# Opening of a two-layer fp32 decoder trunk: five modulation tiles on TensorE, x second in the load queue, conv rows as 128 rows, small loads from ScalarE

## The reference

```
cond = silu(c)
shift, scale, gate = split(cond @ ada_w[layer] + ada_b[layer], 3)
h = rms_norm(x, norm_w[layer]) * (1 + scale) + shift
x = x + gate * branch(h)
```

## Time and profile before

| | us |
|---|---|
| median of 3 runs | 1510.14 (1509.96 to 1510.31) |
| profiled execution | 1509.85, its span 1508.1 |
| TensorE busy | 1446.5 (96%) |
| VectorE busy | 1105.2 (73%) |
| ScalarE busy | 744.5 (49%) |
| take of a modulation tile (L853) | 188.9 for 148, 1.276 each |
| low part of a granule (L834) | 585.5 for 480, 1.222 each |
| DMA | 361.47 MB, mean 240 GB/s |

### The profile page before, as it was taken

The page is one execution under the profiler, slowest core; times in us unless marked ns, Lnnn a source line. Parts: engine busy times, 40 slices in busy tenths (PEclk is TensorE's granted clock), DMA queues, the critical chain, the costliest instruction groups (busy, mean ns, idle before and its releaser), DMA issues.

```text
span 1508.1 us, 19057 instructions
## 1 busy us (share of the span) xinstructions
PE 1446.5 (96%) x6679; PEld 1198.7 (79%) x6679; DVE 1105.2 (73%) x1234; ACT 744.5 (49%) x1002; POOL 41.7 (3%) x78
## 2 busy tenths in 40 slices
PE   2889999999999989899999999999999999999998
PEld 2767888888888867688888888888888888888886
DVE  5999899989898875878766566566566666656657
ACT  3544646454446455544544544544554454554452
POOL 1000110101000000000000000000000000000000
PEclk9999999999999999999999999999999999999999
DMA  9999889998989735798766566556566566566553
GB/s 338 386 393 391 269 282 339 324 327 287 336 294 353 263 114 183 254 310 300 251 184 187 174 191 185 173 189 188 174 194 181 173 191 193 167 189 190 178 182 112
DMA packets 199230, 361.47 MB, mean 240 GB/s; under 512 B 14224, under 2 KB 48360, under 8 KB 199164
## 3 DMA queue, kind: packets, MB, share of 16 engines
q1 hardware_dynamic: 198112, 359.60, 72.3%
q10 hardware_dynamic: 1056, 1.06, 0.2%
HBM read 358.51 MB, written 2.11 MB: 239 GB/s over the span
## 4 chain that ended last, share of the span: by engine, by line
PE 76%; issue 10%; DVE 7%; ACT 3%; DMA 2%; SPq 1%; POOL 0%; ACTq 0%; DVEq 0%; POOLq 0%
PE proj L1336 23%; PE proj L1338 22%; PE proj L1337 22%; DVE ada_acc L853 4%; PE mix L1336 1%; PE mix L1338 1%; PE mix L1337 1%; DVE w_lo L834 1%; DMA raw<-in_att_w_in 1%; DMA ada_more<-in_ada_w 1%; ACT w_hi L563 1%; PE mix L1455 1%; PE mix L1522 1%; PE mix L1570 1%; ACT work L646 1%
## 5 line engine op out<-in xcount | busy, mean ns | idle before, releaser
L834 DVE TENSOR_TENSOR w_lo<-raw,w_hi 128x1024 fp32r<-128x1024 f32 x480 | 585.5, 1222 | 355.5 <-ACT w_hi L563 354.8
L563 ACT ACTIVATE w_hi<-raw 128x1024 fp32r<-128x1024 f32 x480 | 507.4, 1061 | 682.5 <-PE proj L1338 570.5
L1336 PE MATMUL proj<-w_hi,h_hi 128*128 128x512 f32 x1472 | 583.7, 397 | 7.1 <-DVE h_lo L906 3.9
L1338 PE MATMUL proj<-w_hi,h_lo 128*128 128x512 f32 x1472 | 575.2, 391 | 0.0
L1337 PE MATMUL proj<-w_lo,h_hi 128*128 128x512 f32 x1472 | 574.6, 390 | 0.0
L1336 PEld LDWEIGHTS proj<-w_hi,h_hi 128*128 128x128 f32 x1472 | 277.7, 189 | 66.9 <-issue 9.1
L1338 PEld LDWEIGHTS proj<-w_hi,h_lo 128*128 128x128 f32 x1472 | 277.1, 188 | 58.6
L1337 PEld LDWEIGHTS proj<-w_lo,h_hi 128*128 128x128 f32 x1472 | 277.7, 189 | 57.6 <-issue 1.4
L853 DVE SCALAR_TENSOR_TENSOR ada_acc<-ada_raw,cond,ada_acc 128x1024 f32<-128x1024 f32 x148 | 188.9, 1276 | 2.8 <-DMA ada_raw<-in_ada_w 1.8
L1336 PE MATMUL proj<-w_hi,y_hi 128*128 128x512 f32 x320 | 126.0, 394 | 1.3 <-DVE stream L1004 1.3
L1338 PE MATMUL proj<-w_hi,y_lo 128*128 128x512 f32 x320 | 124.6, 389 | 0.0
(11 more groups left out here) (202 smaller groups left out, 936.5 us busy)
## 6 DMA issues: line engine op xcount, KB each, us to landing
raw<-in_mlstm_w_in SPq DMA_DIRECT2D x192, 512.0 KB, 3.7
ada_raw<-in_ada_w SPq DMA_DIRECT2D x160, 512.0 KB, 6.0
raw<-in_att_w_in SPq DMA_DIRECT2D x128, 512.0 KB, 7.1
raw<-in_mlstm_w_in SPq DMA_DIRECT2D x128, 256.0 KB, 3.0
raw<-in_mlstm_w_out SPq DMA_DIRECT2D x64, 512.0 KB, 4.3
raw<-in_att_w_out SPq DMA_DIRECT2D x32, 512.0 KB, 6.1
ada_more<-in_ada_w SPq DMA_DIRECT2D x16, 512.0 KB, 10.9
work<-in_ada_w SPq DMA_DIRECT2D x16, 512.0 KB, 10.6
```

The lines of the kernel that those rows point to most:

```text
L563: act.activation(w_hi[:, c % LEAD, :], raw[:, c % LEAD, :], ACT.Copy).then_inc(hi_ready, 1)
L834: dve.tensor_tensor(w_lo[:, c % LEAD, :], raw[:, c % LEAD, :], w_hi[:, c % LEAD, :].bitcast(F32), ALU.subtract).then_inc(lo_ready, 1)
L1336: pe.matmul(out_, a_hi, b_hi, start=start, stop=False, **kw)
L1338: return pe.matmul(out_, a_lo, b_hi, start=False, stop=stop, **kw)
```

## The change

Four things, all in the first 45 us:

1. Tiles 3, 5, 8, 14 and 15 of block 0 are not taken by VectorE. TensorE multiplies each with its condition column: the tile is the stationary operand, eight pieces of 128x128, and `cond[:, t]` the one moving column (`mod_part`). Each of these groups of eight matmuls has eight columns of its own in `mix[3]`, and VectorE adds the six sets of columns with two reduces in `mod_evac`. SyncE waits for TensorE before it fills such a tile's slot again (`slot_free`).
2. x is loaded second, behind tile 0, and ScalarE squares a chunk as soon as it has landed (a semaphore for each chunk). The normalization stands earlier on VectorE, behind the takes of tiles 2 and 4.
3. The conv weights are loaded as 128 rows of 512 B into 128 partitions, turned with one transpose, and no longer lie in `raw`, so SyncE's wait for `conv_turned` is gone.
4. The five small loads (c, constants, `norm_w`, `mlstm_norm_w`, conv weights) are issued by ScalarE.

The core of the diff:

```diff
-        conv_rows = raw[:].rearrange("p l n -> p (l n)")[0:TAPS, 0:2 * QK1]
+        conv_rows = work[:, 9344:9472]
+        BY_PE = {0: (3, 5, 8, 14, 15)}
+        def slot_free(sp, n):
+            if by_pe(n) and n % KT == KT - 1:
+                sp.wait_ge(ada_summed, n // KT + 1)
+            elif by_pe(n):
+                sp.wait_ge(ada_pe, turned(n + 1))
+            else:
+                sp.wait_ge(ada_tile, taken(n + 1))
         def load_ada(sp, n):
...
-            wait(sp, ada_tile, n + 1 - (ADA_START if n < ADA_LATE + ADA_SLOTS else ADA_SLOTS))
+            before = n - (ADA_START if n < ADA_LATE + ADA_SLOTS else ADA_SLOTS)
+            if before >= 0:
+                slot_free(sp, before)
         def sp_program(sp):
-            sp.dma_start(rows_c, c[0].rearrange("(t p) -> t p", p=P)).then_inc(c_in, 16)
-            sp.dma_start(const[:], consts[:, 0:C_COS]).then_inc(consts_in, 16)
-            sp.dma_start(rows_n, norm_w.rearrange("l (t p) -> (l t) p", p=P)).then_inc(c_in, 16)
+            load_ada(sp, 0)
             sp.wait_ge(bias_zeroed, 1)
-            for n in range(KT):
+            sp.dma_start(ada_bias[0:1], ada_rows[0:1, 0:2, 0:NC]).then_inc(ada_bias_in, 16)
+            for q in range(CHUNKS):
+                sp.dma_start(stream[:, :, q * NC:(q + 1) * NC], x_v[:, :, q * NC:(q + 1) * NC]).then_inc(x_in[q], 16)
+            for n in range(1, KT):
                 load_ada(sp, n)
-                if n == 3:
-                    sp.dma_start(rows_v, mlstm_norm_w[0].rearrange("(t p) -> t p", p=P)).then_inc(rows_in, 16)
-                    sp.dma_start(conv_rows, mlstm_conv_w[0]).then_inc(rows_in, 16)
-                for q in X_AFTER.get(n, []):
-                    sp.dma_start(stream[:, :, q * NC:(q + 1) * NC], x_v[:, :, q * NC:(q + 1) * NC]).then_inc(x_in, 16)
-            sp.wait_ge(conv_turned, 1)
         def act_program(act):
+            act.dma_start(rows_c, c[0].rearrange("(t p) -> t p", p=P)).then_inc(c_in, 16)
+            act.dma_start(const[:], consts[:, 0:C_COS]).then_inc(consts_in, 16)
+            act.dma_start(rows_n, norm_w.rearrange("l (t p) -> (l t) p", p=P)).then_inc(c_in, 16)
+            act.dma_start(rows_v, mlstm_norm_w[0].rearrange("(t p) -> t p", p=P)).then_inc(rows_in, 16)
+            act.dma_start(conv_rows, mlstm_conv_w[0].rearrange("k (j p) -> (k j) p", p=P)).then_inc(rows_in, 16)
         def mod_evac(dve, bank, k, layer, b):
-            dve.tensor_copy(shift_flat[:, at], mix[bank][:, 0:4])
+            scale = mix[bank][:, 4:8]
+            if k in BY_PE:
+                sums = mix[bank][:, 0:8 * (1 + len(BY_PE[k]))].rearrange("p (i j) -> p j i", j=8)
+                scale = scale_sum[:]
+                dve.tensor_reduce(scale, sums[:, 4:8], AX.X, ALU.add).then_inc(scale_added, 1)
+                dve.tensor_reduce(shift_flat[:, at], sums[:, 0:4], AX.X, ALU.add)
+                dve.wait_ge(scale_added, list(BY_PE).index(k) + 1)
         def dve_program(dve):
             for n in range(KT):
-                take_ada(dve, n)
-                if n == 8:
+                if not by_pe(n):
+                    take_ada(dve, n)
+                if n == 0:
                     dve.wait_ge(conv_turned, 1)
...
-                if n == 9:
+                if n == 2:
                     norm_sum(dve, 0)
-                if n == 11:
+                if n == 4:
                     norm_scale(dve, 0)
+        def mod_part(pe, k, t):
+            n = k * KT + t
+            at = 8 * (1 + BY_PE[k].index(t))
+            pe.wait_ge(ada_in[slot_of(n)], slot_fills(n) * 16)
+            for j in range(8):
+                op = pe.matmul(mix[3][:, at + j:at + j + 1],
+                               ada_slot[slot_of(n)][:, j // 4, j % 4 * P:(j % 4 + 1) * P],
+                               cond[:, t:t + 1], start=True, stop=True)
         def pe_program(pe):
             pe.wait_ge(cond_ready, 1)
+            mod_part(pe, 0, 3)
+            mod_part(pe, 0, 5)
             pe.wait_ge(xn_act, CHUNKS)
             pe.wait_ge(xn_dve, CHUNKS)
-            for q in range(UNIT):
+            for q in range(4):
                 turn_x(pe, 0, q)
-            pe.wait_ge(xnT_act, 4)
-            mod_sum(pe, 3, 0, 0)
+            mod_part(pe, 0, 8)
+            for q in range(4, UNIT):
+                turn_x(pe, 0, q)
+            mod_taken(pe, 0)
+            mod_part(pe, 0, 14)
+            mod_part(pe, 0, 15)
```

More of the change, by code:

```diff
@@ L289, in build @@
             "consts_in", "rows_in", "norms_in", "gates_in"))
-        x_in, x_again, ones_set, rows_turned = (sem(n) for n in (
-            "x_in", "x_again", "ones_set", "rows_turned"))
+        x_again, ones_set, rows_turned = (sem(n) for n in ("x_again", "ones_set", "rows_turned"))
+        x_in = [ctx.enter_context(nc.semaphore(f"x_in{q}")) for q in range(CHUNKS)]
         cond_ready, rows_out, masks_ready, rope_table = (sem(n) for n in (
@@ L358, in fills, with by_pe, taken, turned @@
             return it * (BODY // LEAD + sum(n % LEAD == c % LEAD for n in body)) + sum(1 + two_loads(n) for n in same)
+        BY_PE = {0: (3, 5, 8, 14, 15)}
+        def by_pe(n):
+            return n % KT in BY_PE.get(n // KT, ())
+        def taken(n):
+            return sum(not by_pe(i) for i in range(n))
+        def turned(n):
+            return sum(by_pe(i) and i % KT < KT - 1 for i in range(n))
         MOD, GATE = 0, 1
@@ L586, in turn_bank @@
         def turn_bank(layer, q):
-            return mix[q % 4] if layer or q < 4 else proj[q // 2 % 2][q % 2]
+            if layer:
+                return mix[q % 4]
+            return [mix[0], mix[1], mix[2], proj[1][1], proj[0][0], proj[0][1], proj[1][0], mix[0]][q]
         def xnT_evac(act, q):
@@ L842, in take_ada @@
             if t:
-                dve.wait_ge(ada_tile, n)
+                dve.wait_ge(ada_tile, taken(n))
                 other = sum_
@@ L1231, in dve_program @@
                 {i + 1: [lambda k=k: mod_evac(dve, 3, k, 1, k - 4)] for i, k in SUM_MOD1.items()},
[L1232 removed]
+                {i: [lambda n=n: take_ada(dve, n) for n in ns if not by_pe(n)] for i, ns in TAKES0.items()},
                 {-4: [lambda: h_rest(dve, 0, 1)]},
@@ L1430, in turn_rows @@
             pe.transpose(proj[0][1][:, 128:160], rows_v, ident[0:32, 0:32])
-            for j in range(2 * QK1 // P):
-                op = pe.transpose(proj[0][1][:, j * TAPS:(j + 1) * TAPS], conv_rows[:, j * P:(j + 1) * P],
-                                  ident[0:TAPS, 0:TAPS])
-            op.then_inc(conv_turned, 1)
+            pe.transpose(proj[0][1][:, 0:P], conv_rows, ident).then_inc(conv_turned, 1)
         def turn_x(pe, layer, q):
@@ L1439, in turn_x @@
             pe.wait_ge(xn_dve, CHUNKS * layer + q // 2 + 1)
+            if layer == 0 and q == 7:
+                pe.wait_ge(xnT_act, 1)
             if layer and q >= 4:
```

42 lines of the change are left out of this document (27 added, 15 removed).

## The result

| | before | after |
|---|---|---|
| median of 20 executions each | 1510.35 us | 1513.20 us |
| ratio | | 1.0017 [1.0009, 1.0025] |
| profiled execution, its span | 1509.85, 1508.1 | 1509.55, 1507.7 |

Forecast were 1506.2 us and a gain of 3.9. One execution of each set (1648.8 and 2987.0 us) lies far off the others, and the ratio leaves it out. The changed kernel's other executions stand in two clusters: nine at 1509.0 to 1511.9, ten at 1513.0 to 1516.9 us. Of those of before, 18 of 19 stand at 1509.3 to 1511.8, one at 1513.8. The profiled execution of the changed kernel is of the lower cluster.

What follows compares the result with a forecast made beforehand. The weight stream was taken as the limit, with VectorE barely keeping up. Stream gain 3.5 plus 0.4 slack gave 3.9 us off 1509.85, 1505.95; with the median 0.29 higher, 1506.2 us, 8-in-10 range 1504.6 to 1508.4.

Steps and rivals of the forecast that it cites:

- A weight stream at its ceiling: Stages from 58 to 120 us: the DMA engines are busy without a pause at 394 GB/s, taken as the most possible.
- forecast A: Main forecast: the weight stream limits how much of the opening's lead reaches the end; -3.9 us, 1506.2, chance 0.54.
- the 0.47 us between raw 15's two parts: Near 83 us: time from the high part's end to VectorE's read, taken as slack letting VectorE gain 0.4 beyond the stream.
- rival B: VectorE's whole opening lead is kept, by a denser stream or slots never short; -6.3 us, 1503.8, chance 0.10.
- First matmul at 37.8 us: End of the opening: the first projection matmul starts at 37.8 instead of 44.08 us, 6.3 us earlier.
- I price a group at 1.84: Opening on TensorE: each group of eight one-column matmuls costs 1.84 us; three in a row at the end, 5.5 us.
- rival C: TensorE's clock falls in the opening, all three last groups slow, first matmul at 42.0 us; -2.1 us, 1508.0, chance 0.20.
- E, SyncE stands: SyncE waits before tile 16 for group 8 and the stream runs dry; slower, +5.0 us, 1515.1, chance 0.04.
- Stream, start: Before 13 us: earlier first tile gains 1.66 us and short conv rows 1.3, so the stream runs 3.0 us earlier.
- Rival D: The stream's hole at 9 to 13 us is not from the conv rows; -2.6 us, 1507.5, chance 0.12.
- Block 3 keeps its 1.66 us, TensorE leaves with it: Sum of block 3: still 1.66 us behind the last take it needs, so TensorE leaves 3.9 us earlier.

Runs made afterwards that it cites:

- e11: Kernel before with two 128-byte gaps, so everything the stream lands in starts at a multiple of 256 bytes; ratio 0.9995.
- e10: Kernel before with 32 unused bytes a partition ahead of `work`; 1511.06 us, ratio 1.0004.
- e3: Changed kernel with tiles 10 and 12 on TensorE instead of 14 and 15, ahead of the sum; 1510.67 us, ratio 1.0006.
- e1: Changed kernel run again without any edit; 1510.57 us, ratio 1.0001 to the kernel before.
- e8: Changed kernel with the five small loads issued by SyncE again; 1512.33 us, ratio 1.0011.
- e4: Changed kernel with the conv weights as 4 rows of 16 KB again, issued by ScalarE; 1511.5 us, ratio 1.0014.
- e2: Changed kernel with no tile on TensorE, VectorE taking all 16 of block 0; 1510.11 us, ratio 0.9993.
- e14: Changed kernel with tiles 10 and 12 on TensorE instead of 14 and 15, stream destinations at multiples of 256 bytes; 1508.94 us, ratio 0.9991.
- e15: Changed kernel with only tiles 10 and 12 on TensorE, behind the transposes, with 26 fillers, destinations at multiples of 256 bytes; 1505.68 us, ratio 0.9965.
- e16: Changed kernel with only tiles 10 and 12 on TensorE, behind the transposes, with 26 fillers, not aligned; 1511.22 us, ratio 1.0004.
- e12: Changed kernel with everything the stream lands in at a multiple of 256 bytes; ratio 1.0011.
- e17: Repeat of e15: changed kernel, only tiles 10 and 12 on TensorE behind the transposes, fillers, aligned; 1506.57 us, ratio 0.9973.

## Why the prediction was wrong, step by step

Two steps failed: the stream was taken for the limit, and the opening was reckoned 5.6 us too short. The second is what left no gain.

**"A weight stream at its ceiling", the limit of forecast A: wrong.** 394 GB/s was no ceiling (e11: 406) and the stream did not set TensorE's departure: at 406 GB/s the sum of block 2 stands where it stood (118.10). That sum keeps its distance from the first projection matmul instead. Nine of the 20 traces have 74.0 or 74.1 us between them, at 387, 393 and 406 GB/s, and all have 1388.6 to 1391.6 us from the sum to the end. VectorE is busy for 15.9 of 16, 19.9 of 20 and 27.7 of 30 us there, and its pace doesn't change with the rate. That VectorE's list makes the 74 us is read from these rows; no run made the list shorter. Where the stream of e11 gets ahead, SyncE stands for slots that VectorE still has to free: 350 GB/s from 44 to 60 us, 386 in e10.

In the earlier trace rows ScalarE waits 19 times for raw weights; they came late for ScalarE, not for VectorE. I took the 0.47 us between raw 15's two parts for VectorE's whole margin. In e11 the high part comes 1.0 us earlier (82.36 before) and VectorE reads it when it did (83.89 before):

```profile
81.37 1.06 ACT L565 ACTIVATE w_hi<-raw 128x1024 fp32r<-128x1024 f32 x1 [4.09 <-DMA raw<-in_att_w_in]
...
83.86 1.22 DVE L836 TENSOR_TENSOR w_lo<-raw,w_hi 128x1024 fp32r<-128x1024 f32 x1
```

The mechanism itself exists: with the first matmul at 41.3 us VectorE does run into the stream (e3, four waits, 1.1 us). In the changed kernel it never came into play, since VectorE was only 0.7 us ahead. That lead was kept whole, which is rival B's mechanism (0.10).

**First matmul at 37.8 us: wrong by 5.6, the term that cost the gain.** It has two parts. "I price a group at 1.84": the sum and groups 14 and 15 end 8.9 us after the sum's start instead of 5.5, which is 3.4 us. And the sum starts at 32.0 us instead of 29.8. VectorE took its last tile that much later because the tiles came later: raw 0, the transfer behind tile 15, was forecast for 32.4 us, 3.0 earlier than before, and landed at 34.5 (issued at 25.52, 9.0 us to landing), 0.9 earlier.

```profile
34.59 1.06 ACT L585 ACTIVATE w_hi<-raw 128x1024 fp32r<-128x1024 f32 x1 [3.04 <-DMA raw<-in_att_w_in]
```

The first part is rival C's place; it was priced at 42.0 us and is 43.35 or, in the upper cluster, 47.3. C's argument against itself, the clock shown at 1.00 from 17 to 33 us, was a misreading: the earlier trace rows already had the transposes at 3.65 us for 16 in that execution and 2.55 for the next 16. The Trainium skill, "TensorE: Matmul & The Clock Gate", section "The HAM clock gate (the "warmup" mystery)", has the lower level as the default. e1, where nothing in the opening is fast, agrees; why TensorE, marked busy for 27.2 of the 28 us from 17 to 45, did not come up there, no run shows.

**Why the median is 1513.2 and not 1510:** ten of 19 executions are of the upper cluster. The forecast had no term for two clusters.

**E, SyncE stands:** its number was met by luck. In the upper cluster SyncE waits 12.1 us for groups (8.2 in the lower) and then 9 for a granule's slot, the queue is dry at 50 us, and the execution took 1515.86 us; E gave 1515.1, for group 8 ending at 38.5 us. It ended at 31.3, and what is late is the first matmul, 3.3 us later than before, plus 1.2 us more up to the sum of block 2 and 1.5 in the rest.

**Stream, start:** 1.66 + 1.3 us were forecast; 6.20 to 6.30 instead of 5.70 MB by 20 us are 1.3 to 1.5 us at 393 GB/s. The loads on ScalarE give 0.6 to 0.9 (e8), the short rows 0.2 to 0.5 (e4). What made the hole of the earlier trace rows stays open: in before it ends as the four long rows land (13.1 us), but e4's four rows cost only 0.2 to 0.4 us from ScalarE's queue, and 128 short ones in SyncE's queue gave nothing from 5 to 13 us (e8). Rival D, that the hole doesn't go with the rows, was nearer here. The dip at 4 to 8 us takes part of the start back. The lead is 0.19 MB at 110 us, because from 20 us on the changed kernel moves 34.74 MB and before 35.15.

**A step missing altogether:** the new tile `scale_sum`. I counted its instructions, not its 32 bytes ahead of `work`.

**"Block 3 keeps its 1.66 us, TensorE leaves with it": right.** What the sum of block 2 gains or loses stays: -0.74 us at both sums. The trace's 0.4 us at the end instead of 0.74 lie inside the spread of the rest (1388.6 to 1391.6).

**Where the 74.0 us don't hold,** it is the clock in most traces. In e2, e3, e10, e14, e15 and e16 the granted clock is 0.50 from 107 or 108 to 111 us, ScalarE waits 3.7 to 6.4 us for TensorE, and VectorE behind it 1.0 to 1.2; in e8 the same happens at 112 to 116. The nine traces with 74.0 us have 1.00 there. In the six TensorE had stood for 2.95 to 2.99 us just before, but 2.91 us in before brought no fall; what decides it wasn't tried. In e11, e12 and e17 the fall behind the sum of block 2 lasts 7 us instead of 4, and the sum of block 3 comes 45.9 or 46.0 us after it instead of 44.4.

## What to carry to other kernels

Before you call a stream the limit, ask whether its consumer would run on without it: change the rate alone and see if the dates move. Price one-column matmuls by the duration that their neighbours show in the same place, not by the clock column and not by a group elsewhere. When two traces differ by a microsecond, compare the granted clock stretch by stretch before you blame the memory. After adding a tile, however small, look at where those behind it start.
